# A two-block transformer kernel on one core: the softmax scaling of the first block's attention divided between VectorE and ScalarE

## The reference

```python
h = rms_norm(x, norm_mix[l]);  proj = h @ w_in[l]
# q, kc, vc, ks, vs, kw, vw, gates, hq, hf, hi, hg  are split from proj
p_cmp = masked_softmax(sc, ...)    # over 31 compressed positions
p_sel = masked_softmax(ss, ...)    # keys ks; 16 blocks of 64 are chosen of 8, so: all of them, causal
p_win = masked_softmax(sw, ...)    # keys kw; a window of 512, so: causal too
o = g[..., 0:1] * o_cmp + g[..., 1:2] * o_sel + g[..., 2:3] * o_win
```

## Time and profile before

| | |
|---|---|
| median of 3 runs | 1950.91 us (1950.79 to 1950.96) |
| the profiled execution | 1951.39 us |
| its span, first to last instruction | 1949.6 us |
| granted TensorE clock | 1.000 over the span |
| busy: TensorE, weight load, VectorE, ScalarE, GpSimd | 99%, 77%, 47%, 43%, 45% |
| busy in 95 to 345 us (the attention of the first block): VectorE, ScalarE | 194.38 and 146.68 of 250 us |

### The profile page before, as it was taken

The page is one execution under the profiler, slowest core; times in us unless marked ns, Lnnn a source line. Parts: engine busy times, 40 slices in busy tenths (PEclk is TensorE's granted clock), DMA queues, the critical chain, the costliest instruction groups (busy, mean ns, idle before and its releaser), DMA issues. The chain is left out here.

```text
span 1949.6 us, 25556 instructions
## 1 busy us (share of the span) xinstructions
PE 1923.3 (99%) x9142; PEld 1509.9 (77%) x9142; DVE 911.5 (47%) x1421; ACT 836.2 (43%) x1273; POOL 880.4 (45%) x1185
## 2 busy tenths in 40 slices
PE   9999999999999999999999999999999999999998
PEld 7766666888888887777688888887777688888887
DVE  5577877442231355777541313133777643222132
ACT  5456565443342355655532223134555543222233
POOL 4322211556455465343456456454443355454553
PEclk9999999999999999999999999999999999999999
DMA  8211111333233233222133233333222233242322
GB/s 229 65 44 44 33 44 33 88 107 109 87 94 112 81 92 98 76 67 75 55 103 114 81 104 100 85 97 97 76 66 76 65 87 112 84 120 86 109 86 76
DMA packets 318099, 168.50 MB, mean 86 GB/s; under 512 B 15027, under 2 KB 313494, under 8 KB 317846
## 3 DMA queue, kind: packets, MB, share of 16 engines
q1 hardware_dynamic: 314432, 162.38, 29.0%
q10 hardware_dynamic: 3542, 4.50, 0.9%
HBM read 160.29 MB, written 2.10 MB: 83 GB/s over the span
## 5 line engine op out<-in xcount | busy, mean ns | idle before, releaser
L742 POOL TENSOR_TENSOR wlo<-raw,whi 128x256 fp32r<-128x256 f32 x1160 | 863.4, 776 | 1038.0 <-ACT whi L789 1038.0
L1638 PE MATMUL accs<-Xh,whi 128*128 128x512 f32 x1448 | 582.7, 402 | 0.1
L1639 PE MATMUL accs<-Xl,whi 128*128 128x512 f32 x1448 | 564.4, 390 | 0.0
L1641 PE MATMUL accs<-Xh,wlo 128*128 128x512 f32 x1440 | 561.9, 390 | 0.0
L789 ACT ACTIVATE whi<-raw 128x1024 fp32r<-128x1024 f32 x291 | 307.7, 1061 | 264.5 <-PE accs L1641 218.4
L1638 PEld LDWEIGHTS accs<-Xh,whi 128*128 128x128 f32 x1448 | 271.8, 188 | 88.6 <-issue 17.9
L1639 PEld LDWEIGHTS accs<-Xl,whi 128*128 128x128 f32 x1448 | 272.1, 188 | 56.2 <-issue 3.6
L1641 PEld LDWEIGHTS accs<-Xh,wlo 128*128 128x128 f32 x1440 | 270.3, 188 | 58.2
L1638 PE MATMUL accs<-Uh,whi 128*128 128x512 f32 x744 | 289.7, 389 | 0.8 <-DVE xT L1224 0.8
L1641 PE MATMUL accs<-Uh,wlo 128*128 128x512 f32 x744 | 289.4, 389 | 0.0
L1639 PE MATMUL accs<-Ul,whi 128*128 128x512 f32 x744 | 289.4, 389 | 0.0
(11 more groups left out here) (305 smaller groups left out, 1908.9 us busy)
## 6 DMA issues: line engine op xcount, KB each, us to landing
raw<-in_w_ff_dram SPq DMA_DIRECT2D x128, 512.0 KB
raw<-in_w_in_dram SPq DMA_DIRECT2D x71, 512.0 KB
raw<-in_w_gate_up_dram SPq DMA_DIRECT2D x44, 512.0 KB
raw<-in_w_down_dram SPq DMA_DIRECT2D x16, 512.0 KB
raw<-in_w_o_dram SPq DMA_DIRECT2D x16, 512.0 KB
px<-W ACTq DMA_DIRECT2D x64, 64.0 KB, 2.0
raw<-in_w_down_dram SPq DMA_DIRECT2D x8, 384.0 KB
W<-in_x_dram SPq DMA_DIRECT2D x4, 512.0 KB, 6.3
```

The source lines that it names most:

```text
L742: pool.tensor_tensor(lo[:, ks], raw[:, unit_no % RAW, ks], hi[:, ks].bitcast(F32), ALU.subtract).then_inc(sems["wlo"], 1)
L1638: mmul(y, whi[:, slot, k], xh[:, k], start=(i == 0), stop=False)
L1639: last = mmul(y, whi[:, slot, k], xl[:, k], start=False, stop=("both" in u and i == len(ks) - 1))
L1641: last = mmul(y, wlo[:, slot, k], xh[:, k], start=False, stop=(i == len(ks) - 1))
```

## The change

Of the four pieces of each `n2`, VectorE keeps the two of head g = 0, and ScalarE takes the two of head g = 1, each an ACTIVATE with function Copy and the factor as a pointer to a column. ScalarE waits in `n2` for a new semaphore `n_rc`, which VectorE raises after the factors; its second copy raises `n_oa`. TensorE waits in `n3` for `n_ok` and `n_oa`. VectorE waits for the `n_oa` of the `n2` before it writes the factors again. The order of the items stays as it is.

```diff
@@ scalar
+                elif kind == "n2":
+                    _, i, a, h = item
+                    act.wait_ge(sems["n_rc"], at("n_rc", 1))
+                    for n in range(2):
+                        p = probs[2 * h + n][:, 1, 0:P * (2 * h + n + 1)]
+                        A(p, p, ACT.Copy, scale=nrc[:, 2 * n + 1:2 * n + 2]).then_inc(sems["n_oa" if n else "act"], 1)
+                        act.wait_ge(sems["n_oa" if n else "act"], at("n_oa", 1) if n else chained())
@@ vector
                     dve.wait_ge(sems["S_act"], at(f"n1_{h}"))
+                    if begun("n_oa"):
+                        dve.wait_ge(sems["n_oa"], at("n_oa"))
                     dve.reciprocal(nrc, sme[:, c:c + 4]).then_inc(sems["dve"], 1)
...
-                    TTn(v, v, gates_of(i, 1 + a)[:, 2 * h:2 * h + 2], ALU.mult).then_inc(sems["dve"], 1)
-                    dve.wait_ge(sems["dve"], chained())
-                    for n in range(4):
-                        qb, g = 2 * h + n // 2, n % 2
-                        p = probs[qb][:, g, 0:P * (qb + 1)]
-                        TS(p, p, nrc[:, n:n + 1], None, ALU.mult).then_inc(sems["n_ok" if n == 3 else "dve"], 1)
-                        dve.wait_ge(sems["n_ok" if n == 3 else "dve"], at("n_ok", 1) if n == 3 else chained())
+                    TTn(v, v, gates_of(i, 1 + a)[:, 2 * h:2 * h + 2], ALU.mult).then_inc(sems["n_rc"], 1)
+                    dve.wait_ge(sems["n_rc"], at("n_rc", 1))
+                    for n in range(2):
+                        p = probs[2 * h + n][:, 0, 0:P * (2 * h + n + 1)]
+                        TS(p, p, nrc[:, 2 * n:2 * n + 1], None, ALU.mult).then_inc(sems["n_ok" if n else "dve"], 1)
+                        dve.wait_ge(sems["n_ok" if n else "dve"], at("n_ok", 1) if n else chained())
@@ tensor
                     pe.wait_ge(sems["n_ok"], at("p_scaled"))
+                    pe.wait_ge(sems["n_oa"], at("pa_scaled"))
```

More of the change, by code:

```diff
@@ L115 @@
     "cv": dict(pv=1),
-    "n1": dict(S_fill=1, S_dve=1, S_act=1), "n2": dict(n_ok=1),
+    "n1": dict(S_fill=1, S_dve=1, S_act=1), "n2": dict(n_rc=1, n_ok=1, n_oa=1),
     "n3": dict(S_fill=1, S_act=1), "n4": dict(pv=1),
@@ L165, in marks_of @@
     if kind == "n2":
-        return dict(p_scaled="n_ok")
+        return dict(p_scaled="n_ok", pa_scaled="n_oa")
     if kind == "n3":
@@ L509 @@
         "sq", "xh", "xl", "rstd", "cmp_t", "cmp_e", "cmp_c", "g_in", "g_e", "g_ok", "kc_ok", "nq_r", "nq_ok", "si_x", "si_e", "si_ok",
-        "ga_x", "g_ok2", "c_x", "c_e", "c_ok", "n_ok", "n_uh", "p_ok", "pv", "f_ok", "f_ln", "ha_b", "ha_d", "ha_e", "ha_k", "hl_d", "hl_e", "hl_f",
+        "ga_x", "g_ok2", "c_x", "c_e", "c_ok", "n_ok", "n_rc", "n_oa", "n_uh", "p_ok", "pv", "f_ok", "f_ln", "ha_b", "ha_d", "ha_e", "ha_k", "hl_d", "hl_e", "hl_f",
         "o_r", "o_y", "uh", "ul", "u_new", "sb_l", "sb_w", "rp", "y0", "y1", "fin_r", "ld_gain", "yg", "x_sq", "x_sum"]
```

## The result

The changed kernel takes 1960.16 us in the median of 4 runs (1957.82 to 1961.16) against 1950.93 us (1950.79 to 1951.03) of the kernel before on the same chip: ratio 1.0047 with a 95% interval of 1.0032 to 1.0061, slower by 9.2 us or 0.47%. The prediction said slower, by 5.5 us, and its range ended at 1958.3. The profiled execution took 1959.49 us, its span is 1957.7.

What follows compares the result with a forecast made beforehand. TensorE, busy 99% of the span, was taken as the bound. 4.65 (second scaling) + 0.5 (fourth) + 0.4 (pass 3) = 5.5 us gave 1956.4 us against the median; own range 1954.8 to 1958.1, 8-in-10 range 1953.6 to 1958.3.

Steps and rivals of the forecast that it cites:

- Second scaling: Passes 0 to 2: ScalarE's copies end late, so TensorE's `n3` starts later, 1.55 us a pass, 4.65 us in all.
- ScalarE's copies: Copies with a pointer as scale: 0.73, 0.62, 0.51 and 0.40 us for 512, 384, 256 and 128 columns.
- overlap of 93 ns: Between ScalarE's two copies: up to 0.09 us off a pair by the skill's page; chained rows showed none.
- First and third scaling: Passes 0 to 2: ScalarE's 0.94 us fit in its idle time and VectorE's saving ends in a wait: nothing.
- Fourth scaling: Passes 0 to 2: `n3` 0.48 us later, 0.32 regained at the next `hF`; 0.5 us in all, near zero.
- Pass 3: Last pass: `n3` behind the second scaling 1.13 us later, part regained; 0.4 us taken, bounds -0.2 and +1.1.
- TensorE's new wait in each of 32 `n3`: TensorE's added wait in `n3`: taken as nothing; otherwise 0.03 us each, 1 us in all.
- a rival to which I gave 0.12: Delay spreads: fourth scaling keeps 0.48 us, pass 3 its 1.1, new waits cost 1; 8.2 us, 1959.1; chance 0.12.

Runs made afterwards that it cites:

- e3: The changed kernel with only the second scaling of each pass shared, the other twelve on VectorE alone: 1959.36 us, ratio 1.0049 to the kernel before.
- e2: The changed kernel with the second scaling of all four passes on VectorE alone, the other twelve shared: 1952.96 us, ratio 1.0009 to the kernel before.
- e5: The changed kernel with the second scaling moved ahead of `split_hi` and `hD`, the fourth ahead of `fg`, in passes 0 to 2: 1952.89 us, ratio 1.0010.
- e9: The changed kernel, second and fourth scalings moved earlier in passes 0 to 2, pass 3's second on VectorE alone, one counter, no own-last-piece waits: 1949.79 us, ratio 0.9994.
- e1: The kernel before with one more TensorE wait in each `n3`, on a semaphore raised long before: 1952.21 us, ratio 1.0006.
- e8: The changed kernel with both engines raising one counter, so `n3` has three waits, and no engine waiting for its own last piece: 1957.15 us, ratio 1.0026.
- e11: The changed kernel with useless identity products, six before the first and two before the second `n3` of passes 0 to 2: 1958.23 us, ratio 1.0040.
- e10: The changed kernel run again unaltered, on one chip with the runs with useless products: 1958.87 us, ratio 1.0041 to the kernel before.
- e4: The changed kernel with six useless identity products before the first `n3` of passes 0 to 2: 1958.26 us, ratio 1.0038 to the kernel before.
- e7: The kernel before, VectorE alone scaling, with second and fourth scalings moved earlier in passes 0 to 2: 1955.43 us, ratio 1.0019.

## Why the prediction was right and wrong

- **Second scaling: right in mechanism and size.** Predicted 1.55 us a pass, measured 1.50 to 1.52; the copies were put at 1.38 us and took 1.36 to 1.37. e3 against e2 shows that the cost lies here.
- **ScalarE's copies: right.** 512 columns were put at 0.73 us. The groups by shape of after, mean ns of one behind the bar:

```profile
L933 ACT ACTIVATE px<-px,nsm 128x512 f32<-128x512 f32 x8 | 5.8, 722 | 0.3
...
L933 ACT ACTIVATE px<-px,nsm 128x384 f32<-128x384 f32 x8 | 4.9, 614 | 0.8 <-DVE nsm L1356 0.6
```
  The overlap of 93 ns that the Trainium skill gives for ACTIVATEs that follow each other ("ScalarE: Activation LUTs", What ACT_TABLE_LOAD costs) does not show between these two, where the second waits for the first: it starts 0.03 us behind it. It does show where no such wait stands between two operations. In e5, where ScalarE waits for its second copy, the copies end at 109.03 and `split_hi` starts at 109.06; in e9, without that wait, `split_hi` (L798) starts 0.10 us before they end:

```profile
107.30 1.38 ACT L942 ACTIVATE px<-px,nsm 128x384 f32<-128x384 f32 x2
...
108.58 1.04 ACT L798 ACTIVATE whi<-raw 128x1024 fp32r<-128x1024 f32 x1
```
- **First and third scaling: right.** Nothing is late behind them, and what VectorE saves ends in a wait.
- **Fourth scaling: nearly right.** 0.43 to 0.44 us lost, as against 0.48, and 0.22 won back, not 0.32. The 0.10 us of weight load were not recovered: of the 0.39 us for which the load had been idle before `hF`, 0.17 stay, put down to TensorE's issue.
- **Pass 3: the wait right, the remainder too small.** `n3` came 1.18 us later against 1.13, the sum of -0.29 (the gain at the first scaling, as foretold) and +1.47:

```profile
310.99 1.36 ACT L933 ACTIVATE px<-px,nsm 128x384 f32<-128x384 f32 x2
...
312.38 0.59 ACT L917 ACTIVATE W<-S 31x512 f32<-31x512 f32 x1
...
313.22 0.30 PE L1777 MATMUL S<-cst,px 128*128 128x128 f32 x1 [1.31 <-ACT W L917]
```
  Behind the second `hF` 0.56 us of it were left, as foretold (0.5). At the end of the pass there are 0.75, where I took 0.4. e1, which has nothing but the wait, shows 0.18 us twice in this stretch.
- **The step that failed: the wait.** "**TensorE's new wait in each of 32 `n3`** [...] I take nothing, since its sequencer runs ahead of the products." In e1 that holds only where no semaphore is late. e1 measures 0.96 us for the wait, and the `n3` behind `cv` in e8 shows that the number of waits makes it. The price was my own upper bound, and it lay in a rival to which I gave 0.12.
- **The term put at nothing without a reason: the clock.** For the second scaling I took the late start as the whole cost ("it moves with them") and let what follows run as fast as before. In no step and in no rival did TensorE's clock stand. Terms of the kind I summed give 4.51 + 0.45 + 0.64 + 0.21 + 0.75 = 6.6 us, near 1957.5; the lowest runs of the changed kernel are 1957.49 and 1957.67, and e11's profile without a drop is 1957.68. The range held that, so the failed wait alone would not have left it. What left it are drops like that of the profiled execution, 3.41 us at half clock for 1.55 us: 1959.49 - 1.55 = 1957.9. The median of the first measurement, 1960.16, stands 2.7 us over 1957.5 and would take two. Its runs of 1960.83 and 1961.16 have mean clocks of 0.997 and 0.998, but without a trace of them the number of drops is an inference.

What is shown: the drop, its length and its price, in the profiles of after, e3, e5, e8 and e10. That it comes from the new idle time of TensorE is not shown. For it: the five profiles with a drop in the attention each have a wait of about 1.2 us or more, not filled, in the 2.6 us before it; e1 and e2, which have no such wait, scatter by 0.6 and 1.0 us, no more than the kernel before on their chip (1.2), and e3 by 6.0. The profiles of e4 and e11, with the waits of passes 0 to 2 filled, have no drop, but they keep the wait of pass 3 and have none behind it either. Against it: the kernel before, without the wait, scatters by 3.6 us on the chip of e5, e7, e8 and e9, with mean clocks down to 0.998, and e9 has two such runs. Single runs of e4 and e11 are still 2 us above the rest. Only one execution of each kernel has a trace. Why the drop falls in pass 1 in one kernel and in pass 2 in another is open as well.

## What to carry to other kernels

Work handed from an engine that is never late to one that arrives just in time costs its whole duration, whatever the busy shares say; move the item to where both are early, or don't share it. Give a consumer one counter that several producers raise, in place of a further wait. And where a change makes TensorE wait in a new place, look at the granted clock behind it, in more than one execution, before you take the late start for the whole cost.

## What the hardware showed unexpectedly

- A wait on a semaphore raised long ago costs 0.15 us where a neighbouring wait is released late (e1: three places in passes 0 to 2); at other `n3` it costs nothing, or as much and is won back a few us on.
- The granted clock fell to 0.50 for 3.41 us, the same length in after, e3, e5, e8 and e10, 1.8 to 2.6 us after TensorE had been idle for 1.2 to 1.4 us. A second, short idle time (0.16 to 0.51 us) lay before or around the start of the drop in after, e3 and e8, but behind it in e10, and e5 has none. Transposes that start 0.11 us apart then start 0.21 apart. The price of the same 3.41 us was 1.1 us in e5, 1.35 in e10, 1.55 in after, 1.6 in e8 and 1.8 in e3; they fell on different products.
- An ACTIVATE that does not wait for the one before it starts about 0.10 us before that one ends (L798 behind the copies in e9, 108.58 and 108.68); one that waits for it starts 0.03 us after (L789 in e5, 109.06 and 109.03).
